# Output projection of a query tile cut into six pieces over the next tile's slots, and differential values with 64 columns

## The reference

```python
def diff_combine(o, lam_params, subln, layer):            # group C
    o = o.reshape(b, s_len, C_HEADS, 2, C_V)              # 4 heads, 2 softmaxes each, 64 values
    out = o[:, :, :, 0] - lam * o[:, :, :, 1]
    return merge_heads(rmsnorm(out, subln) * (1 - lam_init))

oa = window_attention_sink(...)    # 4 heads, a window of three tiles and the context
ob = dense_attention(...)          # 4 heads, 96 wide
oc = diff_combine(dense_attention(...), ...)   # 8 score maps 32 wide, 4 heads of 64 values
od = dense_attention(...)          # 4 heads, 64 wide
out_lat = concatenate([oa, ob, oc, od]) @ w_out
xl = xl + gt_a * out_lat
```

## Time and profile before

| | |
|---|---|
| Median of 3 runs | 2422.58 us (2421.97 to 2428.11) |
| Profiled execution | 2422.05 us, of which span 2420.3 us |
| PE busy | 2094.7 us, 87% of the span |
| DVE busy | 822.4 us, 34% |
| ACT busy | 503.8 us, 21% |
| Mean granted TensorE clock | 0.961 |

### The profile page before, as it was taken

How to read it: one execution, slowest core, us unless ns; L and a number is a source line. 1 busy time by engine, 2 the same in 40 slices (tenths; PEclk the granted TensorE clock), 3 DMA queues, 4 the chain that set the end, 5 groups by cost and what they waited for, 6 DMA issues and landing times.

```text
span 2420.3 us, 28798 instructions
## 1 busy us (share of the span) xinstructions
PE 2094.7 (87%) x10962; PEld 987.8 (41%) x10962; DVE 822.4 (34%) x2136; ACT 503.8 (21%) x1177; POOL 94.3 (4%) x69
## 2 busy tenths in 40 slices
PE   5999989999838989999999899999994878787976
PEld 3434455656523333333333456466652323232322
DVE  3321365767660120110201432378765001110102
ACT  3200054545321010100100321255441000100000
POOL 1100000000000000000000101000000000000000
PEclk9999999999979999999999999999997999999999
DMA  9774020000057979979889302200004999999995
GB/s 334 292 265 172 1 70 1 1 1 1 1 195 277 373 259 360 358 256 372 309 317 356 129 18 70 70 1 1 1 1 178 367 387 387 387 388 387 387 386 224
DMA packets 238102, 504.63 MB, mean 209 GB/s; under 512 B 11194, under 2 KB 16236, under 8 KB 233500
## 3 DMA queue, kind: packets, MB, share of 16 engines
q1 hardware_dynamic: 233312, 487.00, 55.1%
q0 software_dynamic: 2880, 10.49, 1.2%
q10 hardware_dynamic: 1788, 5.43, 0.6%
HBM read 495.55 MB, written 7.34 MB: 208 GB/s over the span
## 4 chain that ended last, share of the span: by engine, by line
issue 63%; PE 13%; SPq 13%; DMA 6%; DVE 3%; ACT 1%; POOL 0%; POOLq 0%; DVEq 0%; ACTq 0%; PEldq 0%
SPq L377 13%; PE psS L519 9%; DMA arena<-in_w_down 4%; PE psT L519 2%; DMA arena<-in_w_up 1%; DMA arena<-in_w_gate 1%; ACT arena L946 1%; PE psO L519 1%; PE psM L519 1%; DVE idx L1617 0%; DVE arena L1616 0%; DMA arena<-normed_rows,LIU 0%; PE psS L522 0%; DVE arena L1619 0%; DVE X L1671 0%
## 5 line engine op out<-in xcount | busy, mean ns | idle before, releaser
L519 PE MATMUL psS<-arena 128*64 128x512 f32 (+7 forms) x4896 | 1167.1, 565 | 105.2 <-DMA arena<-in_w_down 31.4
L519 PEld LDWEIGHTS psS<-arena 128*64 128x64 f32 (+4 forms) x4896 | 465.7, 154 | 723.8 <-issue 674.3
L519 PE MATMUL psT<-arena 128*64 128x512 f32 (+1 forms) x1536 | 259.9, 595 | 24.2 <-DMA arena<-in_w_up 18.9
L946 ACT ACTIVATE arena<-psS 128x128 f32<-128x128 f32 (+4 forms) x146 | 54.7, 412 | 858.8 <-PE psS L519 824.9
L522 PE MATMUL psT<-ident,arena 128*128 128x128 f32 (+1 forms) x926 | 147.9, 291 | 89.2 <-DVE arena L1527 27.8
L522 PEld LDWEIGHTS psT<-ident,arena 128*128 128x128 f32 (+1 forms) x926 | 106.6, 145 | 170.5 <-issue 88.1
L1513 DVE TENSOR_REDUCE mx<-psS 128x1 f32<-128x768 f32 (+2 forms) x200 | 165.0, 825 | 28.6 <-PE psS L519 27.0
L946 ACT ACTIVATE arena<-psS,nb 128x768 f32<-128x768 f32 (+2 forms) x200 | 159.1, 796 | 71.1 <-DVE nb L1518 69.3
L1679 DVE TENSOR_TENSOR arena<-arena,psS 128x512 f32<-128x512 f32 x16 | 11.0, 688 | 461.9 <-PE psT L519 461.9
L519 PEld LDWEIGHTS psT<-arena 128*64 128x64 f32 (+1 forms) x1536 | 82.1, 123 | 196.7 <-issue 196.7
L519 PE MATMUL psM<-arena 128*128 128x512 f32 x352 | 156.9, 596 | 4.0 <-DVE X L1473 3.0
(11 more groups left out here) (184 smaller groups left out, 1237.6 us busy)
## 6 DMA issues: line engine op xcount, KB each, us to landing
arena<-in_w_gate SPq DMA_DIRECT2D x128, 1024.0 KB, 13.3
arena<-in_w_up SPq DMA_DIRECT2D x128, 1024.0 KB, 12.5
arena<-in_w_down SPq DMA_DIRECT2D x128, 1024.0 KB, 13.6
arena<-in_w_mod SPq DMA_DIRECT2D x34, 1024.0 KB, 6.6
gtb<-in_w_mod SPq DMA_DIRECT2D x14, 1024.0 KB, 6.7
arena<-in_w_in SPq DMA_DIRECT2D x6, 2048.0 KB, 9.2
normed_rows<-arena ACTq DMA_DIRECT2D x10, 512.0 KB, 9.7
arena<-in_w_out SPq DMA_DIRECT2D x8, 512.0 KB, 7.7
```

Source lines behind the costliest of these rows:

```text
L519: return nc.tensor.matmul(o, lhsT, rhs, start=start, stop=stop)
L946: return nc.scalar.activation(o, i, f, **kw)
```

## The change

`O` is cut: its two halves become three pieces each, of 3, 3 and 2 of the 8 products, in slots 4, 5, 6 and 8, 9, 10. The sum stays in bank 7 between pieces. VectorE's multiply and add become jobs of their own, `R`, in slots 7 and 11. The `Q` jobs go from slots 10, 12, 14, 16 to 12, 14, 16, 18. `squares` goes from slot 10 to 13. The value product of group C takes the 64 columns of its own head alone and writes 64 columns of `psO`. After the last tile the pieces run one behind the other, with `R` behind every third.

```diff
-OT_AT, OP_AT, QT_AT = (3,), (5, 8), (10, 12, 14, 16)
+OT_AT, OP_AT, RES_AT, QT_AT = 3, (4, 5, 6, 8, 9, 10), (7, 11), (12, 14, 16, 18)
+PARTS = (range(0, 3), range(3, 6), range(6, 8))
...
             if at in OP_AT:
-                jobs.append(("O", i - 1, OP_AT.index(at)))
+                jobs.append(("O", i - 1, *divmod(OP_AT.index(at), len(PARTS))))
+            if at in RES_AT:
+                jobs.append(("R", i - 1, RES_AT.index(at), 0))
...
+    end = [("T", last, 0, 0)]
+    for r in range(2):
+        end += [("O", last, r, p) for p in range(len(PARTS))] + [("R", last, r, 0)]
...
-                    if not first or r == 3:
+                    if (not first or r == 3) and part == 0:
                         pe.wait_ge(z["me"], mj)
...
-                        for k in range(KD):
+                        for k in PARTS[part]:
                             a = WOUT + k * D + r * 512
                             last = mm(bank(b), ar[:, qn + k * P:qn + (k + 1) * P], ar[:, a:a + 512], k == 0, k == KD - 1)
+                        if part < len(PARTS) - 1:
+                            return
                     last.then_inc(z["mj"], 1)
...
-                                a, b = PT[pv % 3] + n * P, VV + k * 768 + VCOL[u]
-                                last = mm(psO[:, u % 4 * P:(u % 4 + 1) * P], ar[:, a:a + P], ar[:, b:b + P], n == 0, n == len(kt) - 1)
+                                a, b = PT[pv % 3] + n * P, VV + k * 768 + VCOL[u] + 64 * (u % 2)
+                                last = mm(psO[:, u % 4 * 64:(u % 4 + 1) * 64], ar[:, a:a + P], ar[:, b:b + 64], n == 0, n == len(kt) - 1)
...
-                        if slot == 10 and i:
+                        if slot == 13 and i:
                             squares(i - 1)
...
                     mj += 1
-                    if kind == "O":
+                    if kind == "R":
                         dve.wait_ge(z["mj"], mj)
                         g = (0 if t >= TC else 1) * D + r * 512
                         link(V.tensor_tensor(bank(7), bank(7), gtb[:, g:g + 512], ALU.mult))
...
-                                            bankv(6, 0, P, 0, (256, 2), (192, 2), (1, 64)),
+                                            bankv(6, 0, P, 0, (128, 2), (64, 2), (1, 64)),
```

More of the change, by code:

```diff
@@ L115, in attention_plan @@
         if at in QT_AT and i + 1 < len(tiles):
-            jobs.append(("Q", i + 1, QT_AT.index(at)))
+            jobs.append(("Q", i + 1, QT_AT.index(at), 0))
         if i and s < n:
-            if at in OT_AT:
-                jobs.append(("T", i - 1, OT_AT.index(at)))
+            if at == OT_AT:
+                jobs.append(("T", i - 1, 0, 0))
             if at in OP_AT:
-                jobs.append(("O", i - 1, OP_AT.index(at)))
+                jobs.append(("O", i - 1, *divmod(OP_AT.index(at), len(PARTS))))
+            if at in RES_AT:
+                jobs.append(("R", i - 1, RES_AT.index(at), 0))
         mult = None
@@ L126, in attention_plan @@
     last = len(tiles) - 1
-    plan.append((None, None, None, [("T", last, 0), ("O", last, 0), ("O", last, 1)], None))
+    end = [("T", last, 0, 0)]
+    for r in range(2):
+        end += [("O", last, r, p) for p in range(len(PARTS))] + [("R", last, r, 0)]
+    plan.append((None, None, None, end, None))
     return plan
@@ L195, in jobs_through @@
         for j in jobs:
-            n += 1
+            n += j[0] in ("Q", "T") or (j[0] == "O" and j[3] == len(PARTS) - 1)
             if j == job:
@@ L589, in _, with job @@
                 tiles, mj = TILES[l], 0
-                def job(kind, i, r):
+                def job(kind, i, r, part=0):
                     nonlocal mj
+                    if kind == "R":
+                        return
                     t = tiles[i]
@@ L711, in _ @@
                         if slot == 0:
-                            pe.wait_ge(z["me"], jobs_through(PLANS[l], ("Q", i, 3)) if i else len(Q_PLACE))
+                            pe.wait_ge(z["me"], jobs_through(PLANS[l], ("Q", i, 3, 0)) if i else len(Q_PLACE))
                         if s >= 2:
@@ L975, in _, with job @@
                 mj = 0
-                def job(kind, i, r):
+                def job(kind, i, r, part=0):
                     nonlocal mj
                     t = tiles[i]
+                    if kind == "O":
+                        return
                     mj += 1
-                    if kind == "O":
+                    if kind == "R":
                         return
@@ L1105, in squares @@
                 def squares(i):
-                    act.wait_ge(z["me"], jobs_through(PLANS[l], ("O", i, 1)))
+                    act.wait_ge(z["me"], jobs_through(PLANS[l], ("O", i, 1, len(PARTS) - 1)))
                     t = tiles[i]
@@ L1536, in _ @@
                             if i:
-                                dve.wait_ge(z["mj"], jobs_through(PLANS[l], ("T", i - 1, 0)))
+                                dve.wait_ge(z["mj"], jobs_through(PLANS[l], ("T", i - 1, 0, 0)))
                             link(V.reciprocal(view(rr, 0, P, p0 + 8, (2, 4)), view(rs, 0, P, p0 + 8, (2, 4))))
                             V.tensor_tensor(view(ar, 0, P, OS, (128, 2), (64, 2), (1, 64)),
-                                            bankv(6, 0, P, 0, (256, 2), (192, 2), (1, 64)),
+                                            bankv(6, 0, P, 0, (128, 2), (64, 2), (1, 64)),
                                             view(rr, 0, P, p0 + 8, (4, 2), (2, 2), (0, 64)), ALU.mult).then_inc(z["Og"], 1)
```

## The result

| | before | after |
|---|---|---|
| Median | 2425.35 us (2421.97 to 2428.36, 4 runs) | 2459.93 us (2451.02 to 2467.62, 4 runs) |
| Profiled execution | 2422.05 us | 2467.62 us |
| Mean granted clock | 0.961 | 0.945 (the other runs 0.948 to 0.953) |

The change costs 26 to 34 us. I had forecast 2423, with 0.17 for slower; the time lies outside the range of 2408 to 2434.

The account below looks back on a forecast made before the run. TensorE was taken as the bound up to slot 16 and VectorE from slot 17 to the next tile's turn 0. Period terms -1.5, +0.2, +1.2 and other tiles summed to +0.6 us: forecast 2423, own range 2417 to 2429, 8-in-10 range 2408 to 2434.

Parts of the forecast that it names:

- the sum: Whole kernel: gains and losses of all tiles added up to +0.6 us; the profiled 2422.05 became 2422.65.
- It has the same work after slot 11 as now: +0.1 each: Two last tiles, without Q jobs: VectorE, busy 22.88 of 24.76 us, keeps its work after slot 11; +0.1 us each.
- The second layer's first tile: Tile without O, bound by VectorE: removing the first Q job gains only 0.3, the last costs 1.2; +0.9 us.
- rivals 1: Group C's value product: streaming is the bound, so 64 columns halve it (12 matmuls in 0.7 us); 2408 us, chance 0.25.
- rival 3: Group C's value product: load and stream run one behind the other, 0.6 us more each; 2441 us, chance 0.04.
- The 0.41 of the fourth piece: Slot 8: piece 4 waits until R of slot 7 has emptied bank 7; TensorE waits some 0.4 us.
- the stall of 2.63: TensorE's wait for VectorE's copy after slot 17: forecast to remain, still at half clock.
- the second context tile's -0.6: Second context tile: loses waits of 1.39 and 0.70 and 1.2 of Q, gains waits of 1.2, 0.7 and 0.9.
- part three: Slot 17 to next tile's turn 0, VectorE-bound, 19.86 us: the last Q job in slot 18 delays product 11; +1.2.
- The period: Second layer, slot 17 to next tile's slot 17: 68.23 us changes by -0.1, staying at 68.1.
- part one: Turn 0's transposes to slot 11's scores, TensorE-bound, 34.56 us: becomes 33.0, -1.5; cutting O adds no TensorE work.
- Rival 2: The gain from turn 0 to slot 11 is absent, the last Q job still costs 1.2; 2432 us, chance 0.14.

Follow-up runs that it names:

- e10: The changed kernel unaltered, measured a second time and profiled again: 2452.69 us, ratio to before 1.0108.
- e2: The changed kernel with 128 columns again in group C's value product and readout; squares stay in slot 13: 2440.49 us, ratio to before 1.0049.
- e4: The changed kernel with 128 columns again in group C and squares in slot 19: 2438.07 us, ratio to before 1.0049.
- e6: The kernel before with only squares moved from slot 10 to 13: 2432.28 us, ratio to before 1.0020.
- e7: The changed kernel with R in slots 6 and 10 instead of 7 and 11: 2466.13 us, ratio to before 1.0141.
- e14: e4 (128 columns, squares in slot 19) with R in slots 6 and 11 and the last Q job in 19: 2424.87 us, ratio to before 0.9996.
- e11: The changed kernel with 96 columns in group C, 32 of them the other head's: 2445.37 us, ratio to before 1.0080.
- e3: The changed kernel with squares in slot 19 instead of 13, 64 columns kept: 2438.27 us, ratio to before 1.0046.
- e16: The kernel before with Q jobs in slots 12, 14, 16, 18 and squares in 13; O whole, 128 columns: 2445.75 us, ratio to before 1.0074.
- e8: The kernel before with only the Q jobs moved to slots 12, 14, 16, 18: 2436.51 us, ratio to before 1.0038.
- e12: The changed kernel with O whole again, product and residual in slots 5 and 8: 2462.67 us, ratio to before 1.0151.
- the table of eight: All eight combinations of Q slots, squares slot (10 or 13) and 64 or 128 columns, with O whole: medians 0 to +37 us over before.
- e9: The kernel before with 64 columns in group C and squares in slot 13: 2434.04 us, ratio to before 1.0025.
- e15: The kernel before with Q jobs in slots 12, 14, 16, 18 and 64 columns; O whole, squares in 10: 2442.07 us, ratio to before 1.0058.
- e18: e14 with the second half a slot earlier: pieces 4 to 9, R in 6 and 10, Q in 11, 13, 15, 19: 2454.19 us, ratio to before 1.0117.

## Why the prediction was wrong

Three steps failed. By size the clock comes first: some 19 us (with `O` whole; 14 to 21 with the pieces, e10 and after against e2) come with the 64 columns beside the waits that the other edits open. In the order of the sum:

**`squares` has no term.** The change moves it from slot 10 to 13; the prediction's sum counts TensorE's and VectorE's moved work and leaves ScalarE's out. It costs 1.04 us of a middle tile in the changed kernel's order (e2 against e4, 8 us in the whole by these traces, 2.4 by the medians), and 4 to 5 alone on the kernel before (e6). Checking every moved instruction against what is queued behind it would have found it: behind slot 13 stand a copy and an exponential that TensorE takes at once.

**"It has the same work after slot 11 as now: +0.1 each"** for the two last tiles is the second. VectorE has 1.4 us more behind slot 11, since `R` was done two slots and one `O` job earlier before. Measured +1.6 and +1.9 (e4); e7 shows that an earlier slot of `R` doesn't take it off VectorE's path. The delay by the schedule is only 0.3 us in each of the two tiles; the other 1.3 and 1.6 are half clock (shown above), and e14's last tile, with the same wait but less half clock and a first half that is 0.65 shorter, is 0.44 over before. Of e4's 11 us, for which the sum had +0.6, these two tiles hold 3.4. The second layer's first tile (+0.9 in the sum) is 1.9 longer in e4's trace and 0.1 in the changed kernel's, from its first score product to the `T` behind it. What makes the rest stays open.

**The sum had no clock.** Every duration was taken at the clock of its row. The changed kernel's mean clock is 0.945 to 0.956. What 64 columns do to it is seen best in the last tiles. In e2, e11, e3 and after a last tile has the same order of work and the same wait of 1.47 for the exponential, 36.3 to 36.5 us behind `T`; they differ in the columns (128, 96, 64, 64), and e3 also in its squares, in slot 19. The windows are the 14 us from 38.0 behind the `T` of the second layer's last tile, in this order:

```profile
1809.60:1823.60 14.00, 14.00 (x93) 10.93 (x92) 12.18 (x29) 9.68 (x20) 0.00 (x0) 0.88 0.00 1
1817.30:1831.30 14.00, 14.00 (x74) 10.46 (x72) 10.00 (x23) 7.55 (x16) 0.00 (x0) 0.68 0.01 1
1798.40:1812.40 14.00, 14.00 (x57) 9.93 (x56) 9.01 (x21) 5.61 (x11) 0.00 (x0) 0.52 0.00 1
1829.60:1843.60 14.00, 14.00 (x57) 9.93 (x56) 9.04 (x21) 6.69 (x14) 0.00 (x0) 0.52 0.01 1
```

TensorE is busy without a break in all of them, at a granted clock of 0.88, 0.68, 0.52 and 0.52, and does 93, 74, 57 and 57 matmul instructions. e4 (128 columns) has 0.88 in the same window and e10 (64) has 0.52. The tile takes 62.18 us with 128 columns, 64.54 with 96, 67.02 and 67.01 with 64. The first layer's last tile has the same order (62.01, 65.05, 67.58; e10 64.32) but for e3, 61.91, where the clock stays up behind the wait.

Taken over the two attention stages, the changed kernel's trace is 21.3 us longer than e2's: 10.4 of it in the two last tiles, 10.5 from the first score product to the `T` after the first latent tile, 0.4 elsewhere. e10's trace is only 9.7 longer, 7.7 of it in the last tiles.

Whether a wait is followed by a fall is another matter, and the first context tile shows it. Until `T` its work is the same in e3 and after (the first tile has no squares), and the same but for 64 columns in e2. In all three TensorE waits 0.48 for ScalarE. After, then e2, then e3:

```profile
327.08 0.49 PE L525 MATMUL psS<-arena 32*128 32x128 f32 x4 [0.48 <-ACT arena L956]
327.50 0.69 PE L528 MATMUL psT<-ident,arena 128*128 128x128 f32 x2
...
344.01 0.69 PE L528 MATMUL psT<-ident,arena 128*128 128x128 f32 x2
```

```profile
324.76 0.72 PE L525 MATMUL psS<-arena 32*128 32x128 f32 x4 [0.48 <-ACT arena L956]
325.42 0.69 PE L528 MATMUL psT<-ident,arena 128*128 128x128 f32 x2
...
332.84 0.44 PE L528 MATMUL psT<-ident,arena 128*128 128x128 f32 x2
```

```profile
324.03 0.49 PE L525 MATMUL psS<-arena 32*128 32x128 f32 x4 [0.48 <-ACT arena L956]
324.45 0.44 PE L528 MATMUL psT<-ident,arena 128*128 128x128 f32 x2
```

Transposes of 0.44 at full clock (granted 0.98 from 324.03 to 341.50 in e3) take 0.69 at half (0.50 from 327.50 to 344.01 after). After and e2 fall to half clock right behind this wait. With 128 columns the clock is back 8 us later; with 64 it is still at half 17 us later. In e3 it does not fall here, although every instruction of TensorE, VectorE and ScalarE from the layer's first gate product to this point lies where it does in the changed kernel, to 0.02 us. From the wait to `T` it is 20.9 us in e3, 23.6 in e2 and 28.0 after (all three are at half clock in the last 3 us of that). e10 is the changed kernel itself: its clock fell 11 us earlier, was back before the wait and does not fall behind it, and it takes 20.9. So whether the fall comes is not decided by the schedule near it.

These traces alone would put the fall at 2.6 us beside 128-column products and at 7.1 beside 64-column ones. e16 forbids that reading. It has 128 columns and falls behind the same wait, and is at half clock for some 17 us (granted 0.51 from 325.40 to 342.65):

```profile
325.40 0.80 PE L525 MATMUL psS<-arena 32*128 32x128 f32 x4 [0.48 <-ACT arena L956]
...
338.89 0.69 PE L528 MATMUL psT<-ident,arena 128*128 128x128 f32 x2
...
342.65 0.44 PE L528 MATMUL psT<-ident,arena 128*128 128x128 f32 x2
```

It takes 27.8 us to `T`, where e8, which has the same work up to there and doesn't fall, takes 21.1. With 64 columns the clock is at half up to `T` and beyond in all three traces that fall here (after, e7, e12); with 128 it is back after 8 us in one (e2) and 17 in the other (e16).

The changed kernel's window from the wait on (the granted clock is the third last figure):

```profile
327.10:343.30 16.20, 16.20 (x92) 10.83 (x92) 8.40 (x31) 7.19 (x23) 0.00 (x0) 0.51 0.00 1
```

TensorE is busy without a break in it, at a granted clock of 0.51. After and e3 are alike up to the wait and unlike behind it; what sets the fall off isn't shown.

What stays open: that the clock stays down longer with fewer columns is shown by the last tiles, the 96 columns and the table of eight; that it does so because TensorE streams less, the activity of the theories on e9 and e15, is my reading and not shown, for no run here filled its stream up with other work at the same schedule. Where the falls come differs from run to run (2447 to 2468 for the same kernel), and why e3, whose second last tile loses as much as the changed kernel's, has no more than e4's time in the median isn't known.

**What held.** A product with 64 columns takes nearly as long as one with 128 (1.29 us, and 1.29 to 1.34 had been given for it); rivals 1 (0.7) and 3 (1.9) are out. No run shows a load of 128 columns at the 0.107 us that this price takes beside the measured 0.111, nor the 0.05 that rival 3 adds for each matmul. The runs showed loads of 190 to 192 ns in both kernels (1763.3 to 1764.6 after), laid over matmuls that follow each other after 1.34 / 12 = 0.112 us with 128 columns (before) and 1.29 / 12 = 0.108 with 64 (after). That the load sets this pace is my reading of that and not shown by itself: the load is the same in both, and the time hardly follows the columns. The 0.41 of the fourth piece and the stall of 2.63 came as forecast, the second context tile's -0.6 too (47.87 in e4 for 48.44), and part three nearly so (20.86 for 21.06). The period without the squares was right to 0.1 us (68.12), but by luck: part one came out 0.6 too long (33.64 for 33.0) and e4's part three 0.7 too short (20.33 for 21.06), as less of it was at half clock (granted 0.92, against 0.83 before). In part one the pieces of the second half take 2.75, 2.77 and 1.81 us (1744.14, 1750.00 and 1754.33 after), 0.36 more than the 6.97 of the whole job, where I had said that cutting adds nothing; the gaps that I had closed, 0.3, did not close. Rival 2, the slower one, came near e8's time (2432 for 2436.5) by a wait that it didn't name: TensorE waits for the exponential in the place that `Q` left. In the changed kernel the pieces fill that place.

## What to carry to other kernels

List every engine whose order an edit touches, the small steps too, and ask for each what stands behind it and who takes that next: the one line of this diff that had no term cost 2 to 9 us with 128 columns (e4 to e2, e8 to e16) and 15 to 23 beside the pieces with 64, where the sum of all the others came to 0.6. Halving the columns that stream past a 128 x 128 stationary operand saved 0.05 of 1.34 us a product here, and cost some 19 us of the kernel beside the waits: behind the same wait of 1.47 us the second layer's last tile took 67.01 (after) instead of 62.18 (e2). One trace of each kernel is too little to price a fall of the clock: the two of the changed kernel differ by 4.4 us in the first context tile alone (44.19 and 39.77 from the first score product to `T`). And a job that only has to be somewhere belongs behind the last product that another engine waits for, where its own engine stands still anyway.

## What was not expected of the hardware

- The load of 128 x 128 takes 192 ns at full clock and 334 at half, and half the columns gain little at half clock either: 12 matmuls take 2.66 us with 64 columns (e7) and 2.77 with 128 (e4), both at a granted clock of 0.50. The groups of weight loads of the changed kernel, first from 1756.14 to 1771.28 at a granted clock of 1.00, then from 330 to 344 at 0.50; the last column before the idle time is the mean in ns:

```profile
L525 PEld LDWEIGHTS psO<-arena 128*128 128x128 f32 x24 | 2.8, 192 | 0.0
```

```profile
L525 PEld LDWEIGHTS psO<-arena 128*128 128x128 f32 x12 | 2.9, 334 | 0.0
```

- The wait of 0.48 us in the first context tile was followed by half clock in six of the thirteen traces that have it: three of seven with 64 columns, the one with 96, two of five with 128. A wait of 1.27 in a dense stretch was too (e18), and one of 1.47 in one of e4's two last tiles, while one of 1.05 was not (the period above).
- The changed kernel's runs scatter more than those of the kernel before: 2447 to 2468 for ten runs, against 2422 to 2433 for some ninety.
